# Post-norm chains in two halves of 256 tokens, and a GpSimd split that waits for four added chunks, in a two-block transformer kernel

## What is computed

```python
# first block, per layer; m comes from a mixer (MLA attention in layer 0, HGRN2 in layer 1)
h = h + rms_norm(m, norm_gains[layer, 1])                           # post-norm of the mixer
a = rms_norm(h, norm_gains[layer, 2])                               # pre-norm of the MLP
h = h + rms_norm(sq_relu_mlp(a, mlp_w1[layer], mlp_w2[layer]), norm_gains[layer, 3])   # post-norm of the MLP
# then the next layer's mixer, or the second block's first mixer, takes rms_norm(h, ...)

def rms_norm(x, g):
    return x * lax.rsqrt(jnp.mean(x * x, axis=-1, keepdims=True) + EPS) * g
```

## Time and profile before

| | before |
|---|---|
| median of three runs | 2623.22 us (2621.65 to 2623.62) |
| the profiled execution, its own time | 2623.17 us |
| its span, first to last instruction | 2620.7 us |
| TensorE matmul busy | 2578.7 us, 98% |
| TensorE weight load busy | 2103.6 us, 80% |
| GpSimd busy | 1943.6 us, 74% |
| VectorE busy | 1100.3 us, 42% |
| ScalarE busy | 665.7 us, 25% |
| mean granted TensorE clock | 0.995 |

### The profile page before, as it was taken

One profiled execution on the slowest core, in us unless ns is written; L12 is line 12 of the kernel. 1 busy time (PEld: TensorE's weight loads), 2 busy tenths in 40 slices (PEclk: granted clock), 3 DMA queues, 4 the chain that ended last, 5 costly groups with the idle time before them and its releaser, 6 DMA issues.

```text
span 2620.7 us, 32913 instructions
## 1 busy us (share of the span) xinstructions
PE 2578.7 (98%) x11979; PEld 2103.6 (80%) x11979; DVE 1100.3 (42%) x1893; ACT 665.7 (25%) x1115; POOL 1943.6 (74%) x1677
## 2 busy tenths in 40 slices
PE   7999999999999999999999999999999999999999
PEld 6778888887888788888777888888877877888887
DVE  6544221127767422112586442525342232643433
ACT  3442111014444311101356221213112022311111
POOL 6456988886665598888581879787866866988784
PEclk9999999999999999999999999999999999999999
DMA  5122323332221232322220333332322212333231
GB/s 157 53 73 65 113 97 96 96 96 66 72 71 65 65 97 97 96 96 88 73 65 18 97 97 97 97 97 81 97 78 83 90 58 76 97 97 110 83 109 69
DMA packets 287877, 224.27 MB, mean 86 GB/s; under 512 B 13491, under 2 KB 281756, under 8 KB 287644
## 3 DMA queue, kind: packets, MB, share of 16 engines
q1 hardware_dynamic: 287196, 222.44, 27.8%
q10 hardware_dynamic: 576, 0.40, 0.1%
HBM read 220.72 MB, written 2.10 MB: 85 GB/s over the span
## 4 chain that ended last, share of the span: by engine, by line
PE 90%; DVE 6%; ACT 1%; issue 1%; DVEq 0%; DMA 0%; POOL 0%; SPq 0%; ACTq 0%; POOLq 0%
PE proj L618 27%; PE proj L620 27%; PE proj L619 27%; PE aux L2236 1%; PE aux L2041 1%; PE aux L2210 1%; DVE hT L745 1%; PE aux L859 1%; DVE F L742 1%; PE aux L2117 1%; DVE a_lo L707 1%; PE proj L801 1%; PE aux L466 1%; PE proj L1980 0%; PE proj L1981 0%
## 5 line engine op out<-in xcount | busy, mean ns | idle before, releaser
L618 PE MATMUL proj<-a_hi,w_hi 128*128 128x512 f32 x1992 | 797.0, 400 | 0.0
L620 PE MATMUL proj<-a_hi,w_lo 128*128 128x512 f32 x1992 | 778.2, 391 | 0.0
L619 PE MATMUL proj<-a_lo,w_hi 128*128 128x512 f32 x1992 | 777.6, 390 | 0.0
L1287 POOL TENSOR_TENSOR w_hi<-raw,small 128x512 fp32r<-128x512 f32 x373 | 393.2, 1054 | 421.6 <-PE proj L620 334.8
L1294 POOL TENSOR_TENSOR w_hi<-raw,small 128x512 fp32r<-128x512 f32 (+2 forms) x449 | 486.3, 1083 | 185.8 <-PE proj L620 185.4
L1299 POOL TENSOR_TENSOR w_lo<-raw,w_hi 128x512 fp32r<-128x512 f32 (+2 forms) x449 | 591.9, 1318 | 6.0
L1298 POOL TENSOR_TENSOR w_lo<-raw,w_hi 128x512 fp32r<-128x512 f32 x372 | 485.1, 1304 | 29.1
L618 PE MATMUL proj<-g_hi,w_hi 128*128 128x512 f32 x1200 | 470.5, 392 | 1.1 <-DVE g_lo L605 0.6
L620 PE MATMUL proj<-g_hi,w_lo 128*128 128x512 f32 x1200 | 467.6, 390 | 0.0
L619 PE MATMUL proj<-g_lo,w_hi 128*128 128x512 f32 x1200 | 467.4, 389 | 0.0
L618 PEld LDWEIGHTS proj<-a_hi,w_hi 128*128 128x128 f32 x1992 | 375.6, 189 | 83.3 <-issue 5.6
(11 more groups left out here) (294 smaller groups left out, 2324.1 us busy)
## 6 DMA issues: line engine op xcount, KB each, us to landing
raw<-in_mlp_w SPq DMA_DIRECT2D x64, 1024.0 KB, 5.1
raw<-in_f_w_up SPq DMA_DIRECT2D x88, 512.0 KB, 5.0
raw<-in_b_w_in SPq DMA_DIRECT2D x24, 1024.0 KB, 5.2
raw<-in_hgrn_w_in SPq DMA_DIRECT2D x32, 512.0 KB, 4.7
raw<-in_f_w_down SPq DMA_DIRECT2D x16, 1024.0 KB, 5.1
raw<-in_b_w_out SPq DMA_DIRECT2D x8, 1024.0 KB, 5.1
raw<-in_f_w_down SPq DMA_DIRECT2D x8, 768.0 KB, 4.3
raw<-in_a_w_in SPq DMA_DIRECT2D x5, 1024.0 KB, 5.2
```

Source lines behind the costliest of these rows:

```text
L618: pe.matmul(psum[r][:], w_hi[r][:, w], xh, start=k == 0, stop=False)
L619: pe.matmul(psum[r][:], w_hi[r][:, w], xl, start=False, stop=False)
L620: last = pe.matmul(psum[r][:], w_lo[r][:, w], xh, start=False, stop=k == kc - 1)
L1287: first = pool.tensor_tensor(hi[:, 0:n], src[:, 0:n], nothing.to_broadcast([P, n, P]), ALU.subtract)
```

## The change

First, the end of each of the four chains is cut into tokens 0 to 255 and 256 to 511 (`HALVES`): the eighth square, its sum, Ln, Exp, chunk 0's multiply and add, and chunk 0's `a_hi`. In `OutProj` the eighth chunk's copy to `acc` goes from ScalarE to VectorE. In `Mlp` the last add to `acc` is halved, and the sum of the seventh square is made ahead of it. The sums of the halves go to two PSUM banks (`self.bank` and `aux[3]`). The thrown-away matmuls become fewer: 9 instead of 19 behind `OutProj`, 2 and 9 instead of 5 and 15 around the sums in `Mlp`.

Second, in the four stages behind these norms GpSimd waits, before it splits unit 3, until VectorE has added chunk 3 of the post-norm.

```diff
@@ LastDirect
+            def square_half(self, act, src, s):
+                if s == 0:
+                    act.wait_ge(sq_used.sem, self.base + self.chunks - 1 - len(self.tiles))
+                act.activation(self.last[:, HALVES[s]], src[:, HALVES[s]], ACT.Square).then_inc(sq_ready.sem, 1)
...
-                pe.matmul(self.bank[:], ones[:], self.total, start=True, stop=False).then_inc(sq_used.sem, 1)
-                pe.wait_ge(sq_ready.sem, self.base + self.chunks)
-                pe.matmul(self.bank[:], ones[:], self.tiles[(self.chunks - 1) % len(self.tiles)], start=False,
-                          stop=True).then_inc(sq_used.sem, 1)
+                for bank, h in zip(self.banks, HALVES):
+                    last = pe.matmul(bank[:, h], ones[:], self.total[:, h], start=True, stop=False)
+                last.then_inc(sq_used.sem, 1)
+            def sum_half(self, pe, s):
+                h = HALVES[s]
+                pe.wait_ge(sq_ready.sem, self.base + self.chunks + s)
+                pe.matmul(self.banks[s][:, h], ones[:], self.last[:, h], start=False, stop=True).then_inc(sq_used.sem, 1)
+            def root(self, act):
...
+                for s, h in enumerate(HALVES):
+                    act.wait_ge(sq_used.sem, self.base + self.chunks + s)
+                    act.activation(log_ms[:, h], self.banks[s][:, h], ACT.Ln, bias=eps,
+                                   scale=1.0 / self.size).then_inc(logs[s][0], 1)
+                    act.wait_ge(*logs[s])
+                    act.activation(rstd[:, h], log_ms[:, h], ACT.Exp, scale=-0.5).then_inc(roots[s], 1)
@@ LateNorm.act, chunk 0
+                        act.wait_ge(*half)
+                        act.activation(tile(a_hi, 0)[:, HALVES[0]], tile(hT, 0)[:, HALVES[0]], ACT.Identity, ...)
+                        act.wait_ge(*h_at(0))
+                        act.activation(tile(a_hi, 0)[:, HALVES[1]], tile(hT, 0)[:, HALVES[1]], ACT.Identity, ...)
@@ PostNorm.dve
-                dve.wait_ge(*self.norm.ready())
-                for c in range(DC + 1):
+                for s, h in enumerate(HALVES):
+                    scaled, added = (self.scaled, self.added) if s else (self.half_scaled, self.half_added)
+                    dve.wait_ge(*self.norm.half_ready(s))
+                    dve.scalar_tensor_tensor(tmp[0][:, h], tile(acc, 0)[:, h], gain("norm", self.gain_at), rstd[:, h],
+                                             ALU.mult, ALU.mult).then_inc(scaled.sem, 1)
+                    dve.wait_ge(*scaled.at(0))
+                    dve.tensor_tensor(tile(hT, 0)[:, h], tile(hT, 0)[:, h], tmp[0][:, h], ALU.add).then_inc(added.sem, 1)
+                for c in range(1, DC + 1):
@@ Mlp.pe
-                keep_running(pe, 5)
                 self.post.norm.sum(pe)
-                keep_running(pe, 15)
+                keep_running(pe, 2)
+                for s in range(2):
+                    self.post.norm.sum_half(pe, s)
+                keep_running(pe, 9)
@@ Mlp.dve
+                        elif last and m == DC - 1:
+                            for h, done in zip(HALVES, ((self.half_taken.sem, 1), taken(self.st, DC + m))):
+                                dve.tensor_tensor(tile(acc, m)[:, h], bank[:, h], tile(acc, m)[:, h], ALU.add).then_inc(*done)
...
-                        if last and m >= 2:
+                        if last and 2 <= m < DC - 1:
                             self.post.norm.add(dve, m - 1)
+                        if last and m == DC - 2:
+                            self.post.norm.add(dve, m)
@@ OutProj
                 self.post.norm.sum(pe)
-                keep_running(pe, 19)
+                for s in range(2):
+                    self.post.norm.sum_half(pe, s)
+                keep_running(pe, 9)
...
+                dve.wait_ge(sq_ready.sem, self.post.norm.base + DC + 1)
+                dve.tensor_copy(tile(acc, DC - 1), psum[self.st.bank(DC - 1)][:]).then_inc(*taken(self.st, DC - 1))
@@ GpSimd, splitting
+            behind_norm = {st_mlp[0]: post_mla, st_hg: mlp[0].post, st_mlp[1]: post_hg, st_dsa: mlp[1].post}
...
+                            if st in behind_norm and j == RING - 1:
+                                pool.wait_ge(*behind_norm[st].added.at(RING - 1))
```

More of the change, by code:

```diff
@@ L532, in program, with __init__ @@
         class LastDirect(AddedNorm):
+            made = 0
+            def __init__(self, chunks, total, load=False):
+                super().__init__(chunks, total, load=load)
+                Norm.squares += 1
+                self.made = LastDirect.made
+                LastDirect.made += 1
+                self.last, self.banks = self.tiles[(chunks - 1) % len(self.tiles)], (self.bank, aux[3])
+            def square_half(self, act, src, s):
+                if s == 0:
+                    act.wait_ge(sq_used.sem, self.base + self.chunks - 1 - len(self.tiles))
+                act.activation(self.last[:, HALVES[s]], src[:, HALVES[s]], ACT.Square).then_inc(sq_ready.sem, 1)
             def add(self, dve, c):
@@ L688, in column, with act @@
                 return gain(self.gain[0], self.gain[1] + c)
-            def act(self, act, h_at, to=rstd):
+            def act(self, act, h_at, to=rstd, half=None):
                 for c in range(DC):
-                    act.wait_ge(*h_at(c))
-                    act.activation(tile(a_hi, c), tile(hT, c), ACT.Identity, bias=zero,
-                                   scale=self.column(c)).then_inc(self.high.sem, 1)
+                    if half and c == 0:
+                        act.wait_ge(*half)
+                        act.activation(tile(a_hi, 0)[:, HALVES[0]], tile(hT, 0)[:, HALVES[0]], ACT.Identity, bias=zero,
+                                       scale=self.column(0))
+                        act.wait_ge(*h_at(0))
+                        act.activation(tile(a_hi, 0)[:, HALVES[1]], tile(hT, 0)[:, HALVES[1]], ACT.Identity, bias=zero,
+                                       scale=self.column(0)).then_inc(self.high.sem, 1)
+                    else:
+                        act.wait_ge(*h_at(c))
+                        act.activation(tile(a_hi, c), tile(hT, c), ACT.Identity, bias=zero,
+                                       scale=self.column(c)).then_inc(self.high.sem, 1)
                     self.norm.square(act, tile(hT, c), c)
@@ L909, in pe, with act @@
                 turns_from(pe, self.st.turns, block)
-                keep_running(pe, 5)
                 self.post.norm.sum(pe)
-                keep_running(pe, 15)
-            def act(self, act, h_at):
-                self.pre.act(act, h_at)
+                keep_running(pe, 2)
+                for s in range(2):
+                    self.post.norm.sum_half(pe, s)
+                keep_running(pe, 9)
+            def act(self, act, before):
+                self.pre.act(act, before.added.at, half=before.half_added.at(0))
                 act.activation(self.factor, log_ms, ACT.Exp, scale=-1.0).then_inc(self.factor_ready.sem, 1)
@@ L926, in act @@
                 turns(act, self.st.turns, block)
-                for c in range(DC):
+                for c in range(DC - 1):
                     emptied(act, self.st, DC + c, self.st.turns - 1)
                     self.post.norm.square(act, tile(acc, c), c)
+                act.wait_ge(*self.half_taken.at(0))
+                self.post.norm.square_half(act, tile(acc, DC - 1), 0)
+                emptied(act, self.st, 2 * DC - 1, self.st.turns - 1)
+                self.post.norm.square_half(act, tile(acc, DC - 1), 1)
                 self.post.norm.root(act)
@@ L986, in pe @@
                 self.post.norm.sum(pe)
-                keep_running(pe, 19)
+                for s in range(2):
+                    self.post.norm.sum_half(pe, s)
+                keep_running(pe, 9)
             def act(self, act):
-                for m in range(DC):
+                for m in range(DC - 1):
                     bank = arrived(act, self.st, m)
@@ L993, in act @@
                     act.copy(tile(acc, m), bank[:]).then_inc(*taken(self.st, m))
+                bank = arrived(act, self.st, DC - 1)
+                for s in range(2):
+                    self.post.norm.square_half(act, bank, s)
                 self.post.norm.root(act)
```

18 lines of the change are left out of this document (14 added, 4 removed).

## The result

The changed kernel takes 2626.27 us, median of 20 runs (2624.58 to 2628.37), against 2622.66 us (2620.97 to 2626.73, 20 runs) of the kernel before on the same chip: ratio 1.0013, 95% interval [1.0007, 1.0019]. It is slower by a little more than 0.1%, and the interval excludes both zero and 0.2%. The profiled execution has an own time of 2625.92 us and a span of 2623.9 us, 2.75 and 3.2 above the one before.

The account below looks back on a forecast made before the run. TensorE bounds the kernel, waiting on the norm chains and on VectorE, gapless while units 0 to 2 run. Three places at +1.8 us and HGRN2 at +0.5 add +5.9 to 2623.17: 2629.1 us; own range 2626 to 2632, overall 2619 to 2632.

Parts of the forecast that it names:

- Start of the units: TensorE's first real matmul behind each norm: about 1.7 to 1.9 us earlier at MLA and MLPs, 0.5 later behind HGRN2.
- the 0.95 of the collision: Behind MLA, chunk 0's add took 1.64 instead of 0.69 us beside GpSimd's last unit 3 split; 0.95 comes back.
- The wait on GpSimd: Unit 3's four split instructions now meet gapless VectorE: 3.54 us lost at each of three places, 0.89 per instruction.
- Rivals A: Part of the collisions does not reach TensorE; each place costs 1.8 us less, 2623.7 us in all; chance 0.20.
- B: VectorE keeps its pace and GpSimd is held up; only the chain's gain is left, 2618.2 us; chance 0.11.
- C: VectorE and GpSimd lock for whole instructions: 4.7 us a place, bad start behind HGRN2, 2633 us; chance 0.06.
- Nothing moves behind HGRN2: Behind HGRN2 the 3.54 us of collisions only move; the start was put at +0.5 us, bounds -0.8 to +1.0.
- Rival D: Fewer fillers and more stalls lower TensorE's clock, up to 2.2 us at each place, 2637 us; chance 0.03.
- The signs: Behind MLP 0: start 1.9 us earlier, GpSimd's split 7 to 8 us in, VectorE instructions 1.4 to 1.8, waits about 3.3.
- nothing takes them back: At three places the 3.54 us of collisions reach TensorE in full, as all four precede chunk 6's `a_lo`.
- The sum: Four places: +1.8 us behind MLA and each MLP, +0.5 behind HGRN2; together +5.9, giving 2629.1 us.
- the case given 0.38: Outcome "same", a total within 0.2% (5.2 us) of the kernel before; slower had 0.51, faster 0.11.

Follow-up runs that it names:

- e2: Kernel before with only GpSimd's wait added, whole chains and all thrown-away matmuls kept; 2632.44 us, ratio 1.0035.
- e6: Changed kernel with eight thrown-away matmuls ahead of TensorE's wait for chunk 3's `a_lo`, except behind HGRN2; 2625.60 us, ratio 1.0012.
- e9: Kernel before with four more thrown-away matmuls at two waits in the DSA stage's indexer units; 2623.99 us, ratio 0.9999.
- e4: Changed kernel, unit 3's high part split at once, low part after all `a_lo`; behind HGRN2 whole split after chunk 6's `a_lo`; 2617.81 us, ratio 0.9977.
- e5: Changed kernel with GpSimd waiting, before unit 3's whole split, until all eight chunks are added; 2622.29 us, ratio 0.9996.
- e7: e4 with unit 3's low part a chunk earlier and 19 thrown-away matmuls behind HGRN2's sums instead of 9; 2618.33 us, ratio 0.9977.
- e1: Changed kernel without GpSimd's wait, so halved chains with unit 3 split as before; 2624.99 us, ratio 1.0006.

## Why the prediction was right, and where not

- **Start of the units.** Forecast -1.7, -1.9, -1.9 and +0.5, measured -1.79, -2.00, -2.01 and -0.24. The first three are shown, and so is the 0.95 of the collision within the first: the wait alone (e2) starts the units 0.95 us earlier behind MLA and not at all behind the MLPs. HGRN2's was mis-sized, inside its bounds of -0.8 to +1.0: three collisions as forecast, but one of them cost only 0.31, and the halves between them still came a little earlier.
- **The wait on GpSimd.** Forecast 3.54 us a place. e2 has 3.55 and 3.54 behind the MLPs, and 3.01 + 0.95 = 3.96 behind MLA, about as much more as the clock costs there by e6 (0.45). Rivals A and B fall with it, and C (4.7 a place; its own factors give 4.62) as well. By the rule of the Trainium skill's page "SBUF — State Buffer", section "Who interferes with whom", the two exclude each other for whole instructions. The alternation one for one agrees, and the price of 0.89 us each is less than GpSimd's own 1.04 to 1.29. The prediction put the difference down to start-up; no run here shows its reason.
- **Nothing moves behind HGRN2.** The four collisions of unit 3's split only moved, as said: from 907.65 on VectorE took 1.53, 1.41, 1.78 and 1.77 us for the same four instructions. But the forecast for the place was +0.5 and it came to 0.00. That the ledger's column reads +0.55 is luck, since all of it lies ahead of the place. The place itself cannot be read finer than half a us: the kernel before, with nothing changed there, has +0.43 in e9, where the clock fell behind TensorE's wait.
- **Rival D.** It was put at 0.03 with the earlier trace rows against it, and it weighed 1.3 us of idle time, though the prediction's own signs had waits of about 3.3 us. The clock did fall at all four places. Only its price was far below D's 2.2 us: 0.45 behind MLA and none behind the MLPs (e6); behind HGRN2 it was not taken apart. One stretch could not tell that it would stay up: at that very point of the same code it fell in e9, behind a wait of 2.01 us, where it had stayed at 1.00 behind 2.02.

```profile
902.80 1.65 PE L648 MATMUL proj<-a_lo,w_hi 128*128 128x512 f32 x3 [2.01 <-DVE a_lo L707]
```

```profile
902.80:906.20 3.40, 3.40 (x8) 2.72 (x9) 3.37 (x4) 1.01 (x2) 1.08 (x1) 0.50 0.27 55
```

- **The signs.** The chain ahead of the first matmul behind MLP 0 is 2.0 us shorter (1.9 forecast), and four VectorE instructions took 1.41 to 1.77 us, as said. GpSimd's four stand 4.9 to 11.1 us into the three units and not 7 to 8: the add of chunk 3 comes earlier than I reckoned. Behind MLP 0 TensorE's waits for VectorE come to 2.2 us and not 3.3. The rest of the loss lies in matmuls at the lower clock, which look busy. And "nothing takes them back" is not quite so: in unit 3 behind the MLPs TensorE waited 0.62 us for the sum of squares before and 0.22 and 0.16 now.
- **The sum.** Four places: forecast +5.9, measured +5.92, but two errors cancel in it, +2.40 for +1.8 behind MLA and 0.00 for +0.5 behind HGRN2. The total of 2629.1 failed by 3.2 us on the execution's own time, and that is above all the indexer's -3.19, for which the sum had no term: it held every other stage fixed. What else lies outside the four places and between the span and the own time nearly cancels (+0.55, +1.1, -1.1 and -0.5). The measured ratio of 1.0013 lies within 0.2%, the case given 0.38, and not beyond it, which had 0.51; the direction was the forecast's. That the same 3 us explain why the medians differ by 3.6 us and not by 5.9 is an inference: only the profiled executions show it.

## What to carry to other kernels

Two engines that exclude each other want their instructions where the other one idles: look for the stretch in which one of them has no gap, count the other's instructions in it, and move those (e4 and the changed kernel differ only in when these instructions run, and have ratios of 0.9977 and 1.0013). A wait that only says "not at the start" can point at the worst place; release it from the end of the dense stretch, or do ahead of it what fits. And before comparing sums of under 5 us with a total, lay both traces side by side stage by stage, since an untouched stage can move by 3 us, and a stretch that is counted to a place can hold 0.5 to 0.9 us from ahead of it. What a fall of TensorE's clock costs is read from what bounds the stretch behind it: 0.5 us where VectorE was late anyway, 1.5 us where nothing else was.

## What the runs showed that I had not expected

- A VectorE instruction of 256 columns pays as much for a collision as one of 512: from 0.42 to 1.37 and from 0.48 to 1.48 us, against from 0.75 to 1.75. Halving a chain doubles what can be hit.
- GpSimd pays too: its four instructions take 1.40, 1.49, 1.59 and 1.73 us beside VectorE, for 1.04 and 1.29 alone.
- In the changed kernel the granted clock fell to 1.2 GHz after 2.2 us without a matmul at three places and after 3.5 us at the fourth, and matmuls then took 0.63 us for 0.39. It stayed there for about 3.4 us.
- The length of the wait alone does not decide it. The clock fell behind waits of 1.82 and 1.89 us (e5), 2.01 (e9), and 2.03 and 2.04 (e2). It stayed up behind 1.80 (e5), 2.02 (before, and e2 behind MLP 1), 2.18 (e7) and even 2.60 and 2.67 us (e1 behind the MLPs).
- In the indexer, with its two waits of 0.62 and 0.45 us filled or not, it fell in 13 of the 14 profiles, for a stretch of 13.2 to 15.0 us where 11.76 is possible.
